# Recurrent-layer gates multiplied as rounded rows and remainders, with squares, gates and last scores in another order and a packed output, in a six-block fp32 network on one core

## What is computed

```
xb, yb = split(h @ w_in)                       # 2048 channels each
yb = gelu(yb)
xb = conv(xb, width 4) + conv_b                # along time, per channel
r = sigmoid(xg @ w_ga + b_ga)                  # 16 blocks of 128 x 128
i = sigmoid(xg @ w_gx + b_gx)
log_a = -8 * r * softplus(-lam);  a = exp(log_a)
b = sqrt(-expm1(2*log_a)) * (i * xb)
hs = scan(h_t = a_t * h_{t-1} + b_t)
out = (hs * yb) @ w_o
```

## Time and profile before

| | us |
|---|---|
| median of 3 runs | 3077.12 (3076.87 to 3077.71) |
| the profiled execution | 3077.26 |
| its span, first to last instruction | 3075.5 |
| PE busy | 3057.3 (99%) |
| DVE busy | 1841.4 (60%) |
| ACT busy | 1446.8 (47%) |
| POOL busy | 108.9 (4%) |
| mean granted PE clock | 0.998 of full |

### The profile page before, as it was taken

One profiled execution on the slowest core, in us unless ns is written; L12 is line 12 of the kernel. 1 busy time (PEld: TensorE's weight loads), 2 busy tenths in 40 slices (PEclk: granted clock), 3 DMA queues, 4 the chain that ended last, 5 costly groups with the idle time before them and its releaser, 6 DMA issues.

```text
span 3075.5 us, 50379 instructions
## 1 busy us (share of the span) xinstructions
PE 3057.3 (99%) x22018; PEld 2887.6 (94%) x22018; DVE 1841.4 (60%) x2224; ACT 1446.8 (47%) x1660; POOL 108.9 (4%) x127
## 2 busy tenths in 40 slices
PE   9999999999999999999999999999999999999998
PEld 9889999999999999999888888889999999999998
DVE  7765555444445567765565655555786665656664
ACT  5544433333333457755443443446555554544543
POOL 0001000000000011110000000002000000000000
PEclk9999999999999999999999999999999999999999
DMA  6234545555545554455555455554444445444453
GB/s 237 105 104 170 174 174 176 177 178 178 175 168 180 177 185 177 156 206 180 190 192 191 179 193 191 189 187 172 179 144 158 175 169 192 165 168 175 165 178 124
DMA packets 78044, 534.46 MB, mean 174 GB/s; under 512 B 8576, under 2 KB 11136, under 8 KB 15104
## 3 DMA queue, kind: packets, MB, share of 16 engines
q1 hardware_dynamic: 77680, 531.10, 48.6%
q10 hardware_dynamic: 144, 0.15, 0.0%
HBM read 529.11 MB, written 2.10 MB: 173 GB/s over the span
## 4 chain that ended last, share of the span: by engine, by line
PE 97%; DVE 1%; ACT 1%; DMA 1%; issue 0%; SPq 0%; DVEq 0%; ACTq 0%
PE PB L1096 23%; PE PB L1106 17%; PE PB L1105 17%; PE PB L1107 17%; PE PB L1097 12%; PE PB L1100 2%; PE PB L1101 2%; PE PB L1102 2%; PE PB L1169 1%; DMA raw<-in_mla_in 1%; PE PB L1236 0%; PE PB L1257 0%; PE PB L1237 0%; DVE WLt L1668 0%; PE PB L1209 0%
## 5 line engine op out<-in xcount | busy, mean ns | idle before, releaser
L1668 DVE TENSOR_TENSOR WLt<-raw,WHt 128x2048 fp32r<-128x2048 f32 (+2 forms) x506 | 1140.3, 2260 | 802.2 <-ACT WHt L1341 801.6
L1341 ACT ACTIVATE WHt<-raw 128x2048 fp32r<-128x2048 f32 (+2 forms) x506 | 955.9, 1890 | 1161.8 <-PE PB L1107 562.6
L1096 PE MATMUL PB<-Xt,WHt 128*128 128x512 f32 x2624 | 935.6, 394 | 0.0
L1097 PE MATMUL PB<-Xt,WLt 128*128 128x256 f32 x2624 | 736.5, 281 | 0.0
L1105 PE MATMUL PB<-Xt,WHt 128*128 128x272 f32 (+1 forms) x2448 | 708.7, 289 | 2.9 <-ACT S L1479 1.3
L1106 PE MATMUL PB<-Xt,WHt 128*128 128x272 f32 (+1 forms) x2448 | 702.1, 287 | 0.0
L1107 PE MATMUL PB<-Xt,WLt 128*128 128x272 f32 (+1 forms) x2448 | 698.6, 285 | 0.0
L1096 PEld LDWEIGHTS PB<-Xt,WHt 128*128 128x128 f32 x2624 | 492.5, 188 | 97.6
L1106 PE MATMUL PB<-Ht,WHt 128*128 128x272 f32 (+1 forms) x1920 | 547.6, 285 | 0.0
L1105 PE MATMUL PB<-Ht,WHt 128*128 128x272 f32 (+1 forms) x1920 | 546.9, 285 | 0.2 <-DVE Ht L1840 0.2
L1107 PE MATMUL PB<-Ht,WLt 128*128 128x272 f32 (+1 forms) x1920 | 544.5, 284 | 0.0
(11 more groups left out here) (237 smaller groups left out, 2445.1 us busy)
## 6 DMA issues: line engine op xcount, KB each, us to landing
raw<-in_gu SPq DMA_DIRECT2D x176, 1024.0 KB, 4.7
raw<-in_dn SPq DMA_DIRECT2D x88, 1024.0 KB, 4.8
raw<-in_odd_in SPq DMA_DIRECT2D x64, 1024.0 KB, 4.7
raw<-in_even_in SPq DMA_DIRECT2D x52, 1024.0 KB, 4.8
raw<-in_lru_in SPq DMA_DIRECT2D x24, 1024.0 KB, 4.7
raw<-in_mla_o SPq DMA_DIRECT2D x16, 1024.0 KB, 4.7
raw<-in_lru_o SPq DMA_DIRECT2D x16, 1024.0 KB, 4.8
raw<-in_even_o SPq DMA_DIRECT2D x16, 1024.0 KB, 4.7
```

The costliest lines, as they stand in the source:

```text
L1096: t.matmul(o, wh, both, start=first, stop=False)
L1097: m = t.matmul(o[:, 0, :], wl, ah, start=False, stop=last)
L1341: a.activation(hi, r, ACT.Copy).then_inc(s_hi, 1)
L1668: v.tensor_tensor(lo, r, hi.bitcast(f32), sub).then_inc(s_lo, 1)
```

## The change

- `conv(q)` of the recurrent layer now also issues `gate_weights` (ACT copies `gw` rounded into `GH`, DVE writes the remainder `GL`; 512 columns each) ahead of the convolution, and `conv_split` (ACT copies `xc` rounded into `xch`, DVE writes the remainder `xcl`; 544 columns each) behind it.
- `gates` on PE are three fp32r products per block in place of one fp32 product, and wait for `gwl` and `xcl`.
- Pairs 6 and 7: pair 7's `conv` is ahead of `close` too; pair 6's gates stand inside the second unit of pair 7's group; decay, scan of pair 6 and gates, decay of pair 7 come one unit earlier than before.
- SP may reload `gw` once it is split.
- Scores of heads 14 and 15 stand ahead of `pv(12)` and `transposes(13)`.
- `head_in` in the even layer stands ahead of `close` (kA and the four qA groups).
- ACT does one small Sqrt ahead of the last four squares.
- The last multiplication writes to a packed buffer, and the six output transfers read from it.

```diff
@@ MLA, last pair of heads
-            p.after(0, lambda a=a, b=b: (scores(a), scores(b), normed_pair(a)))
+            p.later[p.unit].insert(0, lambda a=a, b=b: (scores(a), scores(b), normed_pair(a)))
@@ recurrent layer, plan
     def conv(q):
+        p.mark("gwh", "gwh", q)
+        p.mark("gwl", "gwl", q)
+        p.step("gate_weights", q)
         p.mark("conv", "conv", q)
         p.step("conv", q)
+        p.mark("xch", "xch", q)
+        p.mark("xcl", "xcl", q)
+        p.step("conv_split", q)
...
-        if q != 6:
+        if q < 6:
             p.close()
         p.step("xb_out", q, g)
...
-        c = -1 if q == 6 else 0
-        if q == 6:
+        c = (0, -2, -1)[max(q - 5, 0)]
+        if q < 6:
+            p.after(0, lambda q=q: conv(q))
+        else:
             conv(q)
             p.close()
+        if q == 6:
+            p.inside(1, 1, lambda: gates(6))
         else:
-            p.after(0, lambda q=q: conv(q))
-        p.after(2 + c, lambda q=q: gates(q))
+            p.after(2 + c, lambda q=q: gates(q))
         p.after(3 + c, lambda q=q: decay(q))
         if q < 7:
             p.after(4 + c, lambda q=q: scan(q))
@@ even layer, plan (kA, and the same for the qA groups)
     g = p.group(4, REGM[:2] + VT, "X", 0, "ln_even")
+    head_in("kA", "kA", g, "ak", [ffn1])
     p.close()
-    head_in("kA", "kA", g, "ak", [ffn1])
@@ PE
             def gates(q):
-                t.wait_ge(*when("conv", q))
-                t.wait_ge(s_gw[q % 2], 16 * (q // 2 + 1))
+                t.wait_ge(*when("gwl", q))
+                t.wait_ge(*when("xcl", q))
...
-                        t.matmul(bank[:, 0:T], gw[q % 2][:, (2 * i + g) * 128:(2 * i + g + 1) * 128], xc[:, i, :],
-                                 start=True, stop=True).then_inc(sems["gate"], 1)
+                        t.matmul(o, GH[:, at], xch[:, i, :], start=True, stop=False)
+                        t.matmul(o, GH[:, at], xcl[:, i, :], start=False, stop=False)
+                        t.matmul(o, GL[:, at], xch[:, i, :], start=False, stop=True).then_inc(sems["gate"], 1)
@@ ACT
+            def gate_weights(q):
+                a.wait_ge(s_gw[q % 2], 16 * (q // 2 + 1))
+                if q:
+                    a.wait_ge(*when("gate", q - 1, 3))
+                a.activation(GH, gw[q % 2], ACT.Copy).then_inc(sems["gwh"], 1)
+
+            def conv_split(q):
+                a.wait_ge(*when("conv", q))
+                a.activation(xch, xc, ACT.Copy).then_inc(sems["xch"], 1)
@@ ACT, last_square at mt == 12
+                    a.activation(RTF[:, 0:1], eps6, ACT.Sqrt)
@@ DVE
+            def gate_weights(q):
+                v.wait_ge(*when("gwh", q))
+                v.tensor_tensor(GL, gw[q % 2], GH.bitcast(f32), sub).then_inc(sems["gwl"], 1)
+
+            def conv_split(q):
+                v.wait_ge(*when("xch", q))
+                v.tensor_tensor(xcl, xc, xch.bitcast(f32), sub).then_inc(sems["xcl"], 1)
@@ DVE and SP, the end
+        flat_out = S[:, 0:16 * NT].rearrange("p (k n) -> p k n", n=NT)
-                    v.tensor_tensor(hq, hq, r.unsqueeze(1)...
+                    v.tensor_tensor(flat_out[:, k0:k1, :], hq, r.unsqueeze(1)...
-                        s.dma_start(dst, h[:, k0:k1, M0:T]).then_inc(s_out, 16)
+                        s.dma_start(dst, flat_out[:, k0:k1, :]).then_inc(s_out, 16)
```

More of the change, by code:

```diff
@@ L689, in make_plan @@
         g = p.group(4, REGM[0:2] + WIDE[2:4], "X")
-        p.close()
         gb, key = ("gp", "Vp")[q % 2], "gA%d" % (q % 2)
         head_in(("qA", q), "q", g, "aq", done("q_done"))
+        p.close()
         halves(g, (2, 3), (gb,), done(key))
@@ L883, in build_program @@
         S = sb("S", 6144)
-        P = sb("P", 2048, f32r)
+        P = sb("P", 2112, f32r)
         PB = [ctx.enter_context(nc.psum_tensor(f"PB{i}", [128, 512], f32)) for i in range(8)]
@@ L952, in build_program @@
         gw = [S[:, 4328:4840], S[:, 4840:5352]]
+        GH, GL, xch, xcl = P[:, 0:512], P[:, 512:1024], two(P[:, 1024:1568]), two(P[:, 1568:2112])
         buf = {n: S[:, 512 * i:512 * (i + 1)] for i, n in enumerate(
@@ L1047, in _ @@
                 elif what == "gates" and a[0] + 2 < 8:
-                    s.wait_ge(*when("gate", a[0], 3))
+                    s.wait_ge(*when("gwl", a[0]))
                     s.dma_start(gw[a[0] % 2], A["gates"][a[0] + 2]).then_inc(s_gw[a[0] % 2], 16)
@@ L1203, in gates @@
             def gates(q):
-                t.wait_ge(*when("conv", q))
-                t.wait_ge(s_gw[q % 2], 16 * (q // 2 + 1))
+                t.wait_ge(*when("gwl", q))
+                t.wait_ge(*when("xcl", q))
                 for i in range(2):
                     for g in range(2):
-                        bank = own("gate", q, 2 * i + g)
-                        t.matmul(bank[:, 0:T], gw[q % 2][:, (2 * i + g) * 128:(2 * i + g + 1) * 128], xc[:, i, :],
-                                 start=True, stop=True).then_inc(sems["gate"], 1)
+                        o, at = own("gate", q, 2 * i + g)[:, 0:T], slice((2 * i + g) * 128, (2 * i + g + 1) * 128)
+                        t.matmul(o, GH[:, at], xch[:, i, :], start=True, stop=False)
+                        t.matmul(o, GH[:, at], xcl[:, i, :], start=False, stop=False)
+                        t.matmul(o, GL[:, at], xch[:, i, :], start=False, stop=True).then_inc(sems["gate"], 1)
             def roots(name, squared, *_):
@@ L1286, in attention @@
                     row_stat(*a)
+                elif what == "gates":
+                    gates(*a)
                 elif what == "mla_pv":
@@ L1625, in _ @@
                     gu_out(*x)
+                elif what == "gate_weights":
+                    gate_weights(*x)
+                elif what == "conv_split":
+                    conv_split(*x)
                 elif what == "gates":
@@ L2169, in finish @@
                     hq = h[:, k0:k1, M0:T]
-                    v.tensor_tensor(hq, hq, r.unsqueeze(1).to_broadcast([128, k1 - k0, NT]), mult).then_inc(sems["done"], 1)
+                    v.tensor_tensor(flat_out[:, k0:k1, :], hq, r.unsqueeze(1).to_broadcast([128, k1 - k0, NT]), mult).then_inc(sems["done"], 1)
             for what, *x in plan.steps:
```

## The result

The changed kernel takes **3090.01 us** as median of 5 runs (3089.75 to 3090.76), against 3077.12: ratio 1.0042, 95% interval 1.0031 to 1.0053. It is slower, by 12.9 us; the forecast was 3092.9, with 3083.5 to 3098.0 as range. The profiled execution took 3089.92.

What follows compares the result with a forecast made beforehand. PE was taken as the bound, busy 3057.3 of 3075.5 us. 3077.26 + 16.4 (recurrent layer) + 2.0 (clock) - 1.0 (MLA) - 1.3 (Sqrt table) - 0.5 (output) + 0 = 3092.9 us, range 3083.5 to 3098.

Steps and rivals of the forecast that it cites:

- Part 1, gates on PE: Recurrent layer: twelve fp32r products replace four fp32 blocks on PE, saving 0.33 us a pair, 2.6 in all.
- Part 2, the ring: Recurrent layer: ACT waiting for DVE's convolution closes a loop of 27.0 us per pair; steady part loses 5.1 us.
- Part 3, pairs 6 and 7: End of recurrent layer: convolution and split ahead of `close` delay later weight splits; the layer in all costs +16.4 us.
- table to exp, 6.14, behind the scan of pair 6: Recurrent layer, ACT's sigmoid step: waits for the scan, then takes 6.14 us from table load to exp.
- Part 4, the clock: Recurrent layer: a PE stand of over 7 us lets the clock fall; taken as +2.0 us.
- Part 5, elsewhere: Outside the recurrent layer: MLA -1.0, `head_in` 0, Sqrt table -1.3, packed output -0.5 us.
- All splits hide: Rival, recurrent layer: only the total work of DVE and ACT counts; 3070.6 us, chance 0.08.
- Only the ring costs: Rival, recurrent layer: pair 7's order hides its work, leaving the +5.1 us loss; 3077.6 us, chance 0.06.
- Only pairs 6 and 7 cost: Rival, recurrent layer: earlier pairs' loop stays under 24.8 us by overlap; 3085.4 us, chance 0.12.
- The output stays in 1 KB rows: Rival, output transfers: descriptors still move 256 floats, 0.5 us less gain; 3093.4 us, chance 0.25.

Runs made afterwards that it cites:

- no_conv_wait: Changed kernel with ACT's 544-column copy reading an always-ready table instead of the convolution's output (computes something else): 3079.73 us.
- late_split: Changed kernel with `conv_split` of pairs 0 to 5 one unit later in the list, same instructions: 3080.97 us.
- no_split_latesqrt: Changed kernel with fp32 gates instead of split ones and without the small early Sqrt: 3073.0 us.
- pe_busy: Changed kernel with 48 more zero-adding products on PE behind pair 7's gates and one more DVE subtraction: 3088.34 us.
- rest_only: Kernel before with only the edits outside the recurrent layer: 3074.14 us.
- no_split: Changed kernel with fp32 gates as before, all other edits kept, including the new order of pairs 6 and 7: 3071.78 us.
- late_old: Changed kernel with the old order of pairs 6 and 7 and `conv_split` one unit later for every pair but 6: 3080.29 us.
- late_part: Changed kernel with gates split only for pairs 0 to 5, `conv_split` one unit later, and fp32 gates for pairs 6 and 7: 3070.36 us.

## Why the prediction was right, and where it was off

**Part 1, gates on PE.** Right: the gates of the first two pairs are 0.33 us closer, and 0.32 in each distance of `no_conv_wait`. The second distance of after, 24.95, has 0.13 of the ring in it.

**Part 2, the ring.** Right in mechanism and size: 26.88 us a pair against 27.0 forecast, gates of pair 5 at 1266.76 against 1268.0 at the earliest (the stages ahead had already given 0.85 of this, which my absolute times left out, so 0.4 is the ring's). At the gates of pair 5 PE was 4.7 us behind (this 0.85 left out), where 5.1 was forecast; it was 5.1 behind only one stand later, so the agreement of these two numbers is in part luck. `late_split` and `no_conv_wait` show that it is ACT's wait with a queue behind it.

**Part 3, pairs 6 and 7.** The step was right, its size too large: +16.4 forecast, 13.7 without the clock (15.9 less the 2.2 below). Three terms were mis-sized, 2.6 us together. The start was early by 0.4 (above). The hand-overs between neighbours were taken about 0.1 too long each; over the chain this makes 0.9. And one term was wrong in kind: "table to exp, 6.14, behind the scan of pair 6". The table load stood ahead of the wait for the scan, so it ran beside DVE's work:

```profile
1290.27 1.28 ACT L1504 ACT_TABLE_LOAD   x1
1293.44 1.62 ACT L1504 ACTIVATE S<-PB,par 128x272 f32<-128x272 f32 x4 [1.88 <-DVE S L1997]
```

From the scan's end to exp's end it is 4.88 us and not 6.2. This holds in this place only: in the tail the load started behind PE's sums, for which its root waits too (3063.16, 3059.37 in `no_split_latesqrt`). Where a load falls has to be read from the timeline each time.

**Part 4, the clock.** +2.0 forecast for one fall. There were two, around the stand of 3.1 us and around that of 5.9 (us, PE busy, PEclk, DMA share, GB/s):

```profile
1283.00:1292.00 9.00, 7.00 (x34) 0.62 0.00 1
1311.00:1320.00 9.00, 6.48 (x36) 0.62 0.54 185
```

The first cost nothing, as I had said of the shorter stands: in `pe_busy` that stretch had a clock of 0.81 and PE was 1.0 us further there, and it still stood until the same split of the last group. The second cost 2.2 in the trace and 1.7 by `pe_busy`.

**Part 5, elsewhere.** MLA -1.02 (forecast -1.0). `head_in` -0.13 (0). Early Sqrt 1.28 in the trace, 1.2 by medians (1.3). Output 0.5 in the traces, not clear by medians (0.5). The profiled execution of after won 0.43 more between the root and DVE's last product, on PE's spread (L1161, four products in 0.77 us where before took 1.20). That is no part of the change: `rest_only`, with the same instructions there, took 1.20. The granted clock over these four products was 0.80 in after and 0.50 in `rest_only`. It is no effect of the layer's stands either: `no_split`, which has none, had 1.00 and took 0.68. Compare the two stretches of before with after's:

```profile
3076.00:3081.00 5.00, 2.75 (x22) 2.41 (x21) 2.93 (x10) 0.68 (x2) 0.00 (x0) 0.87 0.00 0
3081.00:3088.00 7.00, 0.00 (x0) 0.00 (x0) 3.82 (x5) 0.00 (x0) 0.00 (x0) 0.50 0.76 300
```

In place of the load at 3063.16 ACT now has it far ahead, and the root 1.31 behind its square with nothing between:

```profile
3060.80 1.28 ACT L1604 ACT_TABLE_LOAD   x1
...
3078.07 0.26 ACT L1409 ACTIVATE sml<-PB,sml 128x2 f32<-128x2 f32 x1 [1.31 <-PE PB L1134]
```

**The sum again.** 3077.26 + 15.9 - 1.0 - 0.1 - 2.3 = 3089.8, where the profiled execution took 3089.92. The forecast was 3.0 too high: 2.7 from part 3, 0.5 from the tail, -0.2 from the clock.

**The rivals.** *All splits hide*: wrong, the ring is over 24.8. *Only the ring costs*: wrong, pairs 6 and 7 added 10.8 to the ring's 5.1. *Only pairs 6 and 7 cost*: `late_split` comes close to this kernel (its gates are 24.8 to 25.1 apart), and gives 3080.97 where I had 3085.4; my price of the two pairs was too high there as well. *The output stays in 1 KB rows*: wrong. The Trainium skill (page "DMA: Bandwidth & Descriptors", section "Why a DMA increments its semaphore by 16 and not by 1") has one descriptor per contiguous run of the last dimension. The packets fell from 2144 to 864, although the access pattern's last dimension is 256 floats in both kernels. Here rows that follow each other without a gap travel together, and the measurement decides.

## What to carry to other kernels

Ask of every instruction that is added to an in-order engine not how long it is but what it waits for, and what is queued behind it. Two engines at 47% and 60% of the span (69% and 73% in 1120 to 1283) cost 15.9 us in this layer because each waited for the other; in pairs 0 to 5 the same instructions with one wait a unit later gained 1.3 us instead, where they had lost 5.1. Then count each engine's list separately when a step is moved (`late_old` moved a wait off ACT and found a split and a scan in its way on DVE), and try edits one at a time: the best kernel took half of this change.

## What the runs showed of the hardware

- A stand of PE can be paid twice. The one of 5.9 us cost 2.2 more, since the unit behind it ran at 1.2 GHz for 5 us; filling the gap with products of zeros made the kernel 1.7 us faster. The clock that fell around the stand of 3.1 cost nothing, since PE had to wait again behind it.
- The same stand of 1.2 us in the tail left PE's four spread products at 0.68 to 0.77 us in after, `no_split` and `late_old`, and at 1.19 to 1.20 in the other seven kernels with the early Sqrt; the granted clock over them was 1.00 in `no_split`, 0.80 in after and 0.50 in `rest_only` and `late_part`. Behind a stand of 2.5 they always took 1.19 to 1.20. So half a microsecond in one profiled tail is by itself no evidence about an edit.
- Outgoing rows that lie back to back left in packets of up to 4096 B; one took 0.159 us where a packet of 1024 B took 0.046, so a byte of a long packet takes 0.86 of the time.
